# Both delta-rule chains in the same beats: a change to the mixer's order, the stick-breaking sums, two boundary rows and the last adds

## The chip, the cores and the metric

The kernel runs on one core of one Trainium2 chip. The metric is the device time of one execution in microseconds (us), with the median taken over several executions. Engines are named as the profile does: PE is TensorE, DVE VectorE, ACT ScalarE, POOL GpSimd, SP SyncE (here it issues the weight transfers).

## The reference

All matrices are fp32. The input is x, 512 tokens of 1024 channels, and a memory of 256 tokens. Six sublayers follow one another, each as h = h + rmsnorm(y) with y computed from rmsnorm(h):

```
y = hybrid_mixer(rmsnorm(h))            # 4 heads of the gated delta rule, and a conv branch
y = memory_cross_attention(rmsnorm(h), rmsnorm(mem))
y = conv_glu_ffn(rmsnorm(h))
y = retention_chunkwise(...) @ w_out
y = stick_breaking_attention(...) @ w_out     # keys and values from the state before
```

The mixer projects h to queries, keys and values (short conv, silu), gates, decay logits and the conv branch:

```
u, w   = triangular_solve(I + L, ...)   # per chunk of 64 tokens
v_new  = u - w @ S
o      = (q * exp(g)) @ S + attn @ v_new
S      = S * exp(g_last) + (k decayed)^T @ v_new
o      = rmsnorm(o) * silu(gate)
c      = causal_dwconv(glu(cfm), 31 taps); c = silu(layernorm(c))
y      = concat(o, c) @ w_out
```

Stick-breaking weighs key s for query t by sigmoid(z_ts) times the product of (1 - sigmoid(z_tj)) over the keys between them, so it needs suffix sums of log(1 - sigmoid(z)) along the keys.

## The kernel before

**Slabs.** All weights stream as 257 slabs of 128x1024 fp32 (512 KB). SP loads a slab into one of three raw buffers, ACT casts its high part to fp32r (`ahead`, L1280, into one of four buffers sh), DVE forms the low part raw minus high (`low`, L1984, buffers sl), and PE multiplies with the activations, also kept as a high and a low part, in three products per pair of tiles (L499, L500, L501; other places through `one`, L504). The buffer sh of slab n is that of slab n + 4, so the cast of slab n + 4 waits until PE has used slab n. Activations have 512 columns (tokens), or 256 for the memory.

**The order.** Each engine has its own program, and the programs meet at semaphores. The order is written by hand. Side work stands in generators, put into queues (bg, fg, side; gp and tp for taps), and `beat()` at fixed places of each slab runs every queue on to its next `yield`: one tick. A slab over 512 columns has 3 beats, after 9, 18 and 24 of its 24 matmuls; a memory slab 1. `drain()` runs a queue to its end at once.

**The mixer.** 20 slabs make queries, keys and values (12, wqkv) and the conv branch (8, wcfm), then KEYS_GATES follows: eight memory-key slabs mk (256 columns) and four gate slabs, slabs 20 to 31; then slabs 32 to 39 for the memory's values, in `tokens` (the mem tokens are stationary), and the output from slab 40. The delta rule works on two pairs of heads, p = 0 and 1, each a `chain(p)`: transposes, the products of each 64-token chunk, doubling levels of the triangular inverse in tiles of 64x64 (32 PE records for each set), u and w, then eight states, in which S (`ss`) passes from chunk to chunk between PE and DVE. Chain 0 starts after slab 5 and chain 1 after slab 14. `gdn_out(p)` norms a pair of heads: ACT squares, a DVE add, an fp32 PE sum by ONE over sq (128x512), ACT Ln and Exp, DVE scaling.

**Taps.** The conv branch has four channel groups c, each with 31 taps, one a tick. Groups 0 and 2 are made by ACT, which scales a shifted copy into ca0 or ca1 (L1466), and POOL, which adds it to acc (L2976); tap q may be scaled only when the add q-2 is done. Groups 1 and 3 are made by DVE in one instruction a tap, in PSUM (L2194). Group 0 starts after slab 7 and group 2 follows it in the same queue; `mk` slabs tick this queue twice. The queue is drained after slab 31.

**Boundaries.** `boundary(b)` sits between sublayers b and b + 1: y is normed and added to h, h is squared and summed, and its reciprocal root RB, a row of 512 values over all partitions, is needed to scale the next products. Before, PE makes 20 sums of one column with ONE as the moving tile, DVE forms the mean and a diagonal, POOL the power, PE a row by ONE times the diagonal over 512 columns, and DVE copies it to RB.

**Stick-breaking.** For four values of p with two heads each, `weights(p, h)` makes scores, softplus `sp` with high part `split` and low part `spl`, and per block of 128 keys s a suffix sum with the masks LWR (triangle) and ONR (ones), each in a bank of its own; `sp` of the last block enters in fp32.

Of the kernel before, what the change touches and what calls it, by code (L numbers as in the profile page):

```python
# [9 lines left out]
ALU = mybir.AluOpType  # L10
# [156 lines left out]
def program(nc, A, out):  # L167
    root = ExitStack()
    with root:
# [42 lines left out]
        with ExitStack() as ph:  # L212
# [14 lines left out]
            SS = alloc(ph, "ss", [128, 2, 128])  # L227
# [32 lines left out]
        with ExitStack() as ph:  # L260
# [11 lines left out]
            ONR = alloc(ph, "onr", [128, 128], F32R)  # L272
# [87 lines left out]
        def sig(n, step=1):  # L360
# [13 lines left out]
        zero, hvp, yr = sig("zeroed"), sig("h_pool"), sig("y_rstd")  # L374
        cv, cva = sig("conv_tap"), sig("conv_act")
# [16 lines left out]
                   x2h, x2l, sq, sa, cs, ms, pw, dg, rw, rb, hs, zero, hvp, yr, cv, cva, wabh, wabl, lgt, lgp, dcv, dca, vtp, vts,  # L392
# [13 lines left out]
        ONB = ((4, 3), (6, 7))  # L406
        TAP_BANKS, TAP_HOP = (2, 5), 12
        CVB = (0, 1, 2, 3, 5, 0, 0, 1, 0, 1, 0, 1)
# [7 lines left out]
        def tap_sum(c, q):  # L416

            return ACC[:, c, :] if q == 30 else PS[TAP_BANKS[0] if c == 1 and q < TAP_HOP else TAP_BANKS[1]][:]
# [36 lines left out]
        GLB = ((1, 2), (0, 1), (0, 1), (0, 1))  # L455
# [17 lines left out]
        Y_ADD = (1, 2)  # L473

# [10 lines left out]
        def tensor_program(e):  # L485
# [99 lines left out]
            def h_sum(b, k, hf, first):  # L585
# [10 lines left out]
                for tb in range(2):  # L596
# [14 lines left out]
            for _ in range(8):  # L611
                one(PS[7][:, 0:256], SS[:, 0, :], SS[:].rearrange("p a b -> p (a b)"), True, True)
# [68 lines left out]
            def chain(p):  # L681
# [103 lines left out]
                for n in range(8):  # L785
                    tb, par = n // 2, n % 2
                    R, RO = RR[par], RR[1 - par]
                    b = bank(6 + par)
                    pe.wait_ge(*gac[(p, "wq", par)])
                    pe.wait_ge(*(gdv[(p, "s", n - 1)] if n else ggp[(p, "s0")]))  # L790
                    for h in range(2):
                        g = (h * 8 + n) * 128
                        t = one(b[:, h * 128:h * 128 + 128], W2[:, g:g + 128], SS[:, h, :], h == 0, False)
# [15 lines left out]
                    rel[6 + par] = [(gac, (p, "tok", n))]  # L809
                    yield  # L810
                for h in range(2):
                    b = bank(6 + h)
# [5 lines left out]
                rel[6], rel[7] = [(gac, (p, "ot", 0))], [(gac, (p, "ot", 1))]  # L818

            def mem():  # L820
                b = bank(3)
# [6 lines left out]
                rel[3] = [(ms, "mem")]  # L828
# [3 lines left out]
                one(bank(3)[:, 0:256], ONE[:], DG[:, 0:256], True, True).then_inc(*rw("mem"))  # L832
                rel[3] = [(rb, "mem")]
# [9 lines left out]
            bg.add(chain(0))  # L843
# [2381 lines left out]
```

## Time and profile before

| | us |
|---|---|
| median of 3 runs | 1701.21 |
| lowest and highest | 1700.98, 1704.16 |
| the profiled execution | 1702.69 |
| its span in the profile | 1700.9 |
| mean granted TensorE clock | 0.997 |
| PE busy | 1679.8 |
| DVE busy | 1051.8 |
| ACT busy | 733.3 |
| POOL busy | 191.6 |

The rows further down come from this one execution; times in them count from its span's start. Matmuls are pipelined, so the duration of one is longer than its distance to the next; distances between starts say what it costs. An fp32 matmul shows as two records.

### The profile page before, as it was taken

To read this page: it belongs to the slowest core of one execution; us is meant where nothing else is said; L and a number is where in the kernel's file an instruction comes from. 1 tells how busy PE (TensorE), PEld (TensorE's weight loads), DVE (VectorE), ACT (ScalarE), POOL (GpSimd) and SP (SyncE) were. 2 spreads that over 40 slices of the span, in tenths; PEclk is the share of its full clock that TensorE was granted. 3 is DMA by queue.
4 is the path that set the end of the run, shared out by engine and by line. 5 is a ranking of instruction groups with operands and counts; after the bars stand their busy time and mean duration, and the time that the engine had idled before them with its cause. 6 is when DMAs were issued, how large, how long until landed. Compare 5 with 4: busy or idle time off the path is not lost.

```text
span 1700.9 us, 23339 instructions
## 1 busy us (share of the span) xinstructions
PE 1679.8 (99%) x9481; PEld 1410.6 (83%) x9481; DVE 1051.8 (62%) x1574; ACT 733.3 (43%) x1125; POOL 191.6 (11%) x165
## 2 busy tenths in 40 slices
PE   9999999999999999999999999999999999999997
PEld 7787887987898888888888888888898888888886
DVE  7889787474389449549575642655475545364545
ACT  6654467643543223213543323323364655353462
POOL 0455461200210000000100000000100000000001
PEclk9999999999999999999999999999999999999999
DMA  6211134421123323323322313213212222222221
GB/s 217 63 39 63 51 100 134 139 75 50 64 73 112 111 75 112 99 80 106 118 88 78 98 53 106 100 64 110 72 62 87 63 86 75 87 75 85 76 74 50
DMA packets 45578, 147.70 MB, mean 87 GB/s; under 512 B 5024, under 2 KB 8992, under 8 KB 45472
## 3 DMA queue, kind: packets, MB, share of 16 engines
q1 hardware_dynamic: 45472, 146.21, 25.9%
q8 instruction: 76, 1.25, 0.3%
q14 instruction: 30, 0.25, 0.0%
HBM read 144.09 MB, written 2.10 MB: 86 GB/s over the span
## 4 chain that ended last, share of the span: by engine, by line
PE 89%; DVE 8%; issue 1%; ACT 1%; POOL 0%; DVEq 0%; ACTq 0%; POOLq 0%
PE ps L499 22%; PE ps L504 22%; PE ps L501 22%; PE ps L500 22%; DVE sl L1984 1%; DVE y L2399 1%; DVE ps L2044 1%; DVE xl L2416 1%; DVE h L2409 0%; PE ps L1119 0%; DVE ps L2194 0%; DVE ps L2038 0%; DVE pad L2036 0%; ACT xh L1325 0%; ACT sh L1280 0%
## 5 line engine op out<-in xcount | busy, mean ns | idle before, releaser
L1280 ACT ACTIVATE sh<-raw 128x1024 fp32r<-128x1024 f32 x257 | 268.0, 1053 | 381.5 <-PE ps L501 256.2
L1984 DVE TENSOR_TENSOR sl<-raw,sh 128x1024 fp32r<-128x1024 f32 x257 | 321.3, 1258 | 126.2 <-ACT sh L1280 126.1
L499 PE MATMUL ps<-xh,sh 128*128 128x512 f32 (+1 forms) x664 | 264.8, 399 | 0.0
L501 PE MATMUL ps<-xl,sh 128*128 128x512 f32 (+1 forms) x664 | 254.3, 383 | 0.0
L500 PE MATMUL ps<-xh,sl 128*128 128x512 f32 (+1 forms) x664 | 254.2, 383 | 0.0
L499 PE MATMUL ps<-sh,xh 128*128 128x512 f32 x384 | 152.5, 397 | 0.0
L500 PE MATMUL ps<-sh,xl 128*128 128x512 f32 x384 | 149.6, 390 | 0.0
L501 PE MATMUL ps<-sl,xh 128*128 128x512 f32 x384 | 149.6, 390 | 0.0
L499 PEld LDWEIGHTS ps<-xh,sh 128*128 128x128 f32 x664 | 125.1, 188 | 27.0 <-issue 3.3
L501 PEld LDWEIGHTS ps<-xl,sh 128*128 128x128 f32 x664 | 125.1, 188 | 25.0
L500 PEld LDWEIGHTS ps<-xh,sl 128*128 128x128 f32 x664 | 125.3, 189 | 23.0 <-issue 1.2
L2907 POOL TENSOR_TENSOR dg<-dg,sq 128x512 f32<-128x512 f32 (+1 forms) x27 | 30.1, 1113 | 816.5 <-ACT sq L1286 815.1
L499 PE MATMUL ps<-x2hu,sh 128*128 128x256 f32 (+1 forms) x346 | 118.9, 344 | 0.0
L501 PE MATMUL ps<-x2lu,sh 128*128 128x256 f32 (+1 forms) x346 | 115.9, 335 | 0.0
L500 PE MATMUL ps<-x2hu,sl 128*128 128x256 f32 (+1 forms) x346 | 115.1, 333 | 0.0
L499 PE MATMUL ps<-x2hd,sh 128*128 128x512 f32 (+1 forms) x300 | 104.2, 347 | 0.0
L501 PE MATMUL ps<-x2ld,sh 128*128 128x512 f32 (+1 forms) x300 | 102.4, 341 | 0.0
L500 PE MATMUL ps<-x2hd,sl 128*128 128x512 f32 (+1 forms) x300 | 102.0, 340 | 0.0
L2976 POOL TENSOR_TENSOR acc<-acc,ca 128x512 f32<-128x512 f32 x60 | 86.1, 1435 | 70.4 <-ACT ca L1466 65.9
L501 PEld LDWEIGHTS ps<-sl,xh 128*128 128x128 f32 x384 | 72.1, 188 | 15.5
L499 PEld LDWEIGHTS ps<-sh,xh 128*128 128x128 f32 x384 | 72.1, 188 | 15.3 <-issue 0.5
L500 PEld LDWEIGHTS ps<-sh,xl 128*128 128x128 f32 x384 | 72.2, 188 | 15.2 <-issue 0.5
(418 smaller groups left out, 3337.5 us busy)
## 6 DMA issues: line engine op xcount, KB each, us to landing
raw<-in_wup SPq DMA_DIRECT2D x44, 512.0 KB, 3.5
raw<-in_wdn SPq DMA_DIRECT2D x24, 512.0 KB, 3.5
raw<-in_rqk SPq DMA_DIRECT2D x16, 512.0 KB, 3.9
raw<-in_rv SPq DMA_DIRECT2D x16, 512.0 KB, 3.5
raw<-in_rg SPq DMA_DIRECT2D x16, 512.0 KB, 4.7
raw<-in_rout SPq DMA_DIRECT2D x16, 512.0 KB, 3.5
raw<-in_sv SPq DMA_DIRECT2D x16, 512.0 KB, 3.4
raw<-in_sg SPq DMA_DIRECT2D x16, 512.0 KB, 3.4
```

Source lines behind the costliest of these rows:

```text
L499: e.matmul(dst, wh, ah, start=start, stop=False, skip_group_check=True)
L500: e.matmul(dst, wl, ah, start=False, stop=False, skip_group_check=True)
L501: return e.matmul(dst, wh, al, start=False, stop=stop, skip_group_check=True)
L504: return e.matmul(dst, a, b, start=start, stop=stop, skip_group_check=True)
L1280: e.activation(SH[j % NSPL][:], RAW[j % NRAW][:], ACT.Copy).then_inc(*hi(j))
L1984: e.tensor_tensor(SL[j % NSPL][:], RAW[j % NRAW][:], SH[j % NSPL][:].bitcast(F32), ALU.subtract).then_inc(*lo(j))
L2044: e.scalar_tensor_tensor(C[:], PAD[:, 1 + q:1 + q + T], prm("gconv", tile * 4 + q), C[:], ALU.mult, ALU.add).then_inc(*cv((n, "t", q) if q ...
L2399: e.scalar_tensor_tensor(Y[:, k, c], Y[:, k, c], prm(gpost[0], gpost[1] + k), YR[:, c], ALU.mult, ALU.mult).then_inc(*yv(("y", b, "n", k, ...
L2416: e.scalar_tensor_tensor(lo_[:, k, c], H[:, k, c], prm(g[0], g[1] + k), hi_[:, k, c].bitcast(F32), ALU.mult, ALU.subtract).then_inc(*s2((k ...
L2907: e.tensor_tensor(SA[:, c], SA[:, c], SQ[(k - 1) % 2][:] if k < 4 else half(SQ, k % 4), ALU.add).then_inc(*sa(("y", b, k)))
L2976: e.tensor_tensor(ACC[:, c, :], ACC[:, c, :], gpb[("tmp", c, q)], ALU.add).then_inc(*tpp((c, q)))
```

## The change

There are five parts.

1. **Order of the weights.** All 12 wqkv slabs come first (0 to 11), then the 8 wcfm slabs (12 to 19). Both chains are added after slab 10 and tick in the same beats, 37 ticks each. Each has its state `SSP[p]` and its own PSUM banks. Both are drained before slab 29, and both `gdn_out` are queued there; before, `gdn_out(0)` was queued before slab 30, chain 1 was drained after slab 31 and `gdn_out(1)` queued then.
2. **Taps** follow the wcfm slabs: group 0 starts after slab 13 (before 7), group 1 after 15 (before 9), group 2 behind group 0 in the same queue, group 3 after slab 19.
3. **Stick-breaking sums.** They run from s = 2 to 0 in one bank that keeps its sum, with the masks UPR (one minus LOW) and LWR; DVE reads the bank between two steps, and PE waits for that. `weights(p)` holds both heads of p, with a tick between the steps.
4. **Rows at boundaries 1 and 2** (H_ROW). PE makes the row at once, 10 fp32 sums by ONE over 256 columns, and ACT does Ln and Exp straight into RB. The one-column sums, the diagonal, the fp32 row and the copy go there.
5. **The last adds.** Of the second half's eight residual adds POOL does k = 0, 2, 4, PE k = 1, 3, 5 (IDN times h plus IDN times y, fp32, ACT copies the sum out), DVE 6 and 7; before, POOL did three and DVE five.

Over the whole program PE has 8481 matmuls where it had 8519, ACT 15 instructions more (among them four more loads of its function table), DVE 9 less, POOL 2 less.

The core of the diff:

```diff
     for p in range(2):
         o += [("wqkv", j * 4 + 2 * p + h) for j in range(3) for h in range(2)]
-        for c in (2 * p, 2 * p + 1):
-            o += [("wcfm", 4 + c), ("wcfm", c)]
+    for c in range(4):
+        o += [("wcfm", 4 + c), ("wcfm", c)]
...
+            SSP = [alloc(ph, f"ss{i}", [128, 2, 128]) for i in range(2)]
...
+        TAP_BANK, JOIN, HEADS_OUT = 7, 10, 9
...
+        OUT_POOL, OUT_PE = (0, 2, 4), {1: 1, 3: 2, 5: 4}
+        H_ROW = (1, 2)
...
+                if b in H_ROW:
+                    t = one(bank(7)[:, 0:256] if hf else PS[4][:, 0:256], ONE[:], hsq(k), first, k == (0 if hf else 6))
...
             slab(5, X, "x", beats=3, at_bank=[0])
             rel[0] = [(cva, conv_tile(5))]
-            bg.add(chain(0))
+            for n in range(6, 12):
+                slab(n, X, "x", beats=3, at_bank=[CVB[n]])
+                rel[CVB[n]] = [(cva, conv_tile(n))]
+                if n == JOIN:
+                    bg.add(chain(0))
+                    fg.add(chain(1))
...
-            glu(0, 6)
+            glu(0, 12)
             side.add(mem())
-            glu(1, 8)
-            rel[TAP_BANKS[0]] = [(tpd, (1, TAP_HOP))]
-            for n in range(6, 12):
-                slab(4 + n, X, "x", beats=3, at_bank=[n % 2])
-                rel[n % 2] = [(cva, conv_tile(n))]
-                if n == 10:
-                    fg.add(chain(1))
+            glu(1, 14)
             glu(2, 16)
             glu(3, 18)
...
             for i, (kind, n) in enumerate(KEYS_GATES):
-                if i == 10:
+                if i == HEADS_OUT:
+                    bg.drain()
+                    fg.drain()
                     side.add(gdn_out(0))
+                    side.add(gdn_out(1))
...
-            fg.drain()
-            fg.add(gdn_out(1))
...
+            def sums(p, h):
+                b, b3 = bank(4), bank(5)
+                last = SP[:, SOFF[3]:]
...
+                one(b[:, 384:T], ONE[:], last, True, False)
+                for s in (2, 1, 0):
+                    pe.wait_ge(*sta[("sh", p, h)])
+                    pe.wait_ge(*stv[("sl", p, h)])
+                    if s < 2:
+                        pe.wait_ge(*stv[("c", p, h, s + 1)])
+                    for q, m in ((s + 1, UPR), (s, LWR)):
+                        for part in (SPLIT, SPL) if q < 3 else ():
...
+            def h_rstd(b, hf):
...
+                e.activation(RB[:, TH[hf]], PS[7 if hf else 4][:, 0:256], ACT.Ln, scale=1.0 / 1024, bias=EPB[:]).then_inc(
...
+                e.activation(RB[:, TH[hf]], RB[:, TH[hf]], ACT.Exp, scale=-0.5).then_inc(*yr(("h", b, hf)))
...
+            for k, i in OUT_PE.items():
+                pe.wait_ge(*hv[(4, k, 1)])
+                one(bank(i)[:, 0:256], IDN[:], H[:, k, TH[1]], True, False)
```

Three places show what the change makes of the order. On PE in the mixer, before, one interruption of the slab products (ss and u_xq belong to chain 0's state, u_rq, u_r and u_t to chain 1's inverse):

```order
L504 MATMUL ps<-ss,u_xq 128x128 x2
L504 MATMUL ps<-u_rq,u_r 64x64 x16
L499 MATMUL ps<-xh,sh 128x512
L500 MATMUL ps<-xh,sl 128x512
L501 MATMUL ps<-xl,sh 128x512
```

And after, with both chains at the same level of the inverse (u_xq, u_x, km are chain 0's):

```order
L507 MATMUL ps<-u_xq,u_x 64x64 x16
L507 MATMUL ps<-u_rq,u_r 64x64 x16
L502 MATMUL ps<-xh,sh 128x512
L503 MATMUL ps<-xh,sl 128x512
L504 MATMUL ps<-xl,sh 128x512
```

Pieces of unlike kind stood together before; now the same piece of both chains does.

On ACT at the end of the key and gate slabs, before. The first row of sh is the cast of slab 33, the next ones that of slabs 34 and 35 and so on; the four rows of qk are chain 1's last copies:

```order
L1280 ACTIVATE sh<-raw 128x1024
L1421 ACTIVATE qk<-ps 64x2x128
L1435 ACTIVATE qk<-ps 128x4x64 x4
L1545 ACTIVATE sq<-qk 128x512 x2
L1280 ACTIVATE sh<-raw 128x1024
L1553 ACTIVATE dg<-ps,epq 128x512
```

After, from the cast of slab 34 over that of 35 to that of 36:

```order
L1306 ACTIVATE sh<-raw 128x1024
L1623 ACT_TABLE_LOAD
L1623 ACTIVATE gt<-gt 128x512
L1502 ACTIVATE ca<-cp,prm 128x512 x2
L1306 ACTIVATE sh<-raw 128x1024
L1502 ACTIVATE ca<-cp,prm 128x512 x16
L1580 ACTIVATE sq<-qk 128x512 x2
L1306 ACTIVATE sh<-raw 128x1024
```

Sixteen taps (ca) stand between the cast of slab 35 and the squares of heads 2 and 3 (sq from qk). On PE the sum over those squares, before, stands behind 18 matmuls of slab 32:

```order
L499 MATMUL ps<-sh,x2hu 128x512
L500 MATMUL ps<-sh,x2lu 128x512
L501 MATMUL ps<-sl,x2hu 128x512
L504 MATMUL ps<-sq,one 128x512 x2
L499 MATMUL ps<-sh,x2hu 128x512
```

After, it stands behind the first six matmuls of slab 32, the last memory-key product (x2hu, x2lu of 256 columns) being ahead of those:

```order
L504 MATMUL ps<-x2lu,sh 128x256
L502 MATMUL ps<-sh,x2hu 128x512
L503 MATMUL ps<-sh,x2lu 128x512
L504 MATMUL ps<-sl,x2hu 128x512
L502 MATMUL ps<-sh,x2hu 128x512
L503 MATMUL ps<-sh,x2lu 128x512
L504 MATMUL ps<-sl,x2hu 128x512
L507 MATMUL ps<-sq,one 128x512 x2
```

On PE in the stick-breaking stage, before, the sums of s = 0 and s = 1 in one tick:

```order
L504 MATMUL ps<-split,lwr 128x512
L504 MATMUL ps<-split,onr 128x384
L504 MATMUL ps<-split,onr 128x256
L504 MATMUL ps<-spl,lwr 128x512
L504 MATMUL ps<-spl,onr 128x384
L504 MATMUL ps<-spl,onr 128x256
L504 MATMUL ps<-sp,one 128x128
L504 MATMUL ps<-split,lwr 128x384
L504 MATMUL ps<-split,onr 128x256
L504 MATMUL ps<-spl,lwr 128x384
L504 MATMUL ps<-spl,onr 128x256
L504 MATMUL ps<-sp,one 128x128
```

After, the sums of s = 3 and 2, of 1, and of 0, with twelve slab products between each:

```order
L507 MATMUL ps<-sp,lwr 128x128
L507 MATMUL ps<-sp,one 128x128
L507 MATMUL ps<-split,lwr 128x256
L507 MATMUL ps<-spl,lwr 128x256
...
L507 MATMUL ps<-split,upr 128x256
L507 MATMUL ps<-spl,upr 128x256
L507 MATMUL ps<-split,lwr 128x384
L507 MATMUL ps<-spl,lwr 128x384
...
L507 MATMUL ps<-split,upr 128x384
L507 MATMUL ps<-spl,upr 128x384
L507 MATMUL ps<-split,lwr 128x512
L507 MATMUL ps<-spl,lwr 128x512
```

A block's sum is now added to what the bank holds, and is not made anew for each s.

## Rows read from the trace of the kernel before

**Rows 1.** The page: busy us of engines; the chain that ended last.

```profile
PE 1679.8 (99%) x9481; PEld 1410.6 (83%) x9481; DVE 1051.8 (62%) x1574; ACT 733.3 (43%) x1125; POOL 191.6 (11%) x165
PE 89%; DVE 8%; issue 1%; ACT 1%; POOL 0%; DVEq 0%; ACTq 0%; POOLq 0%
```

**Rows 2.** PE's waits: who waited for whom, us in total, times, longest.

```profile
PE ps L504 <- DVE sl L1984: 1.7, 4, 0.8
PE ps L701 <- DVE u_xq L2099: 1.3, 1, 1.3
...
PE ps L504 <- DVE km L2111: 1.1, 1, 1.1
```

**Rows 3.** Timeline of PE, stick-breaking sums: start us, us, instruction.

```profile
1313.93 0.28 PE L504 MATMUL ps<-spl,lwr 128*128 128x256 f32 x1
1314.05 0.38 PE L504 MATMUL ps<-sp,one 128*128 128x128 f32 x2
1314.27 0.39 PE L504 MATMUL ps<-sp,lwr 128*128 128x128 f32 x2
```

**Rows 4.** Timeline of PE, first boundary.

```profile
362.26 0.50 PE L504 MATMUL ps<-one,acc 128*128 128x1 f32 x4
362.62 0.36 PE L499 MATMUL ps<-xh,sh 128*128 128x256 f32 x1
...
365.75 1.13 PE L504 MATMUL ps<-dg,one 128*128 128x512 f32 x2
...
366.94 0.40 PE L500 MATMUL ps<-xh,sl 128*128 128x512 f32 x1
```

**Rows 5.** Timeline of DVE, one of the last adds.

```profile
1694.20 0.41 DVE L2877 TENSOR_TENSOR h<-h,y 128x256 f32<-128x256 f32 x1
```

**Rows 6.** Timeline of PE: slab matmuls around one set of 32 records, and around two.

```profile
72.67 0.39 PE L501 MATMUL ps<-xl,sh 128*128 128x512 f32 x1
...
74.40 0.39 PE L500 MATMUL ps<-xh,sl 128*128 128x512 f32 x1
...
75.33 0.40 PE L501 MATMUL ps<-xl,sh 128*128 128x512 f32 x1
...
78.01 0.40 PE L500 MATMUL ps<-xh,sl 128*128 128x512 f32 x1
```

**Rows 7.** Timeline of PE behind w; busy us by engine in 120:121, PEclk (0.50).

```profile
115.49 3.74 PE L504 MATMUL ps<-km,u_xq 64*128 64x64 f32 x32
...
119.75 0.63 PE L500 MATMUL ps<-xh,sl 128*128 128x512 f32 x1
120.00:121.00 1.00, 1.00 (x3) 0.74 (x3) 0.00 (x0) 1.00 (x3) 0.00 (x0) 0.50 0.67 270
```

**Rows 8.** POOL's tap adds: ns min/median/max, first and last start; last row: timeline.

```profile
L2976 POOL TENSOR_TENSOR acc<-acc,ca x2: 1281/1289/1297, 225.2 to 226.7; 128x512 f32<-128x512 f32 x2
L2976 POOL TENSOR_TENSOR acc<-acc,ca x2: 1292/1294/1297, 247.5 to 248.9; 128x512 f32<-128x512 f32 x2
247.46 12.53 POOL L2976 TENSOR_TENSOR acc<-acc,ca 128x512 f32<-128x512 f32 x7 [3.35 <-ACT ca L1466]
```

**Rows 9.** Timeline of PE: slab 32 begins, the output begins.

```profile
267.56 0.48 PE L499 MATMUL ps<-sh,x2hu 128*128 128x512 f32 x1
...
292.93 0.40 PE L504 MATMUL ps<-x2hd,sh 128*128 128x512 f32 x1
```

**Rows 10.** Timeline of ACT: a tap, a cast.

```profile
256.13 0.72 ACT L1466 ACTIVATE ca<-cp,prm 128x512 f32<-128x512 f32 x1 [0.62 <-POOL acc L2976]
265.04 1.05 ACT L1280 ACTIVATE sh<-raw 128x1024 fp32r<-128x1024 f32 x1
```

**Rows 11.** Timeline of DVE: a tap, x2ld of k = 3, a low part.

```profile
251.76 0.76 DVE L2194 SCALAR_TENSOR_TENSOR ps<-cp,prm,ps 128x512 f32<-128x512 f32 x1
...
296.88 0.68 DVE L2326 TENSOR_TENSOR x2ld<-gt,x2hd 128x512 fp32r<-128x512 f32 x1
...
303.06 1.22 DVE L1984 TENSOR_TENSOR sl<-raw,sh 128x1024 fp32r<-128x1024 f32 x1
```

More of the change, by code:

```diff
@@ L416, in tap_sum @@
         def tap_sum(c, q):
[L418 removed]
+            return ACC[:, c, :] if q == 30 else PS[TAP_BANK][:]
         RS = (DG[:], PAD[:, 0:T])
@@ L1191, in values @@
+                yield from sums(p, 1)
             def values(p, h):
@@ L1233, in tensor_program @@
                 bg.drain()
-                for part in (weights, values):
-                    for h in range(2):
-                        bg.add(part(p, h))
+                bg.add(weights(p))
+                for h in range(2):
+                    bg.add(values(p, h))
                 j += 4
@@ L1486, in scalar_program @@
             ahead(10)
-            bg.add(chain(0))
+            conv_act(4)
+            beat(3)
+            conv_act(5)
+            for n in range(6, 12):
+                beat(2)
+                ahead(n + 5)
+                if n == JOIN:
+                    bg.add(chain(0))
+                    fg.add(chain(1))
+                beat()
+                conv_act(n)
             def glu(c, j):
-                if c == 0:
-                    conv_act(4)
-                beat(2 if c == 2 else 3)
+                beat(2 if c == 0 else 3)
                 ahead(j + 5)
-                if c == 0:
-                    conv_act(5)
                 ac.wait_ge(*glv[(c, "sg")])
@@ L1501, in glu @@
                     gp.add(taps_gp(c))
-            glu(0, 6)
+            glu(0, 12)
             side.add(mem())
-            glu(1, 8)
-            for n in range(6, 12):
-                beat(2 if n > 6 else 3)
-                ahead(9 + n)
-                if n == 10:
-                    fg.add(chain(1))
-                beat()
-                conv_act(n)
+            glu(1, 14)
             glu(2, 16)
@@ L1930, in scalar_program @@
                 bg.drain()
-                for part in (weights, values):
-                    for h in range(2):
-                        bg.add(part(p, h))
+                bg.add(weights(p))
+                for h in range(2):
+                    bg.add(values(p, h))
                 j += 4
@@ L2228, in vector_program @@
             conv(4, 4, 5, beat)
-            bg.add(chain(0))
             conv(5, 5, 0, beat)
             low(9)
+            for n in range(6, 12):
+                beat(2)
+                if n == JOIN:
+                    bg.add(chain(0))
+                    fg.add(chain(1))
+                conv(n, n, CVB[n], beat)
+                low(n + 4)
             def glu(c, j):
@@ L2253, in glu @@
                     tp.add(taps(c))
-            glu(0, 6)
+            glu(0, 12)
             side.add(mem())
-            glu(1, 8)
-            for n in range(6, 12):
-                beat(2 if n > 6 else 3)
-                if n == 10:
-                    fg.add(chain(1))
-                conv(n, 4 + n, n % 2, beat)
-                low(8 + n)
+            glu(1, 14)
             glu(2, 16)
@@ L2827, in vector_program @@
                 bg.drain()
-                for part in (weights, values):
-                    for h in range(2):
-                        bg.add(part(p, h))
+                bg.add(weights(p))
+                for h in range(2):
+                    bg.add(values(p, h))
                 j += 4
@@ L2993, in pool_program @@
             beat(3)
-            bg.add(chain(0))
-            for c in range(2):
+            for n in range(6, 12):
+                beat(3)
+                if n == JOIN:
+                    bg.add(chain(0))
+                    fg.add(chain(1))
+            for c in range(4):
                 beat(6)
@@ L3000, in pool_program @@
                     gp.add(taps(c))
-            for n in range(6, 12):
-                beat(3)
-                if n == 10:
-                    fg.add(chain(1))
-            for c in (2, 3):
-                beat(6)
-                if c in ON_GP:
-                    gp.add(taps(c))
-            bg.drain()
             side.drain()
```

288 lines of the change are left out of this document (172 added, 116 removed).

## Prediction

> **What bounds the kernel now.** I read the page's busy shares and its chain first. TensorE is busy 99% of the span and carries 89% of the chain that ended last, DVE 8% [rows 1]. So one matmul less is worth its start-to-start time, and an edit on another engine is worth something only where TensorE waits for it. The list of TensorE's waits [rows 2] says where it does: no entry is over 1.7 us, and those of the mixer are a few tenths to 1.3 us each. A gain can thus come only from fewer or better placed TensorE instructions; a loss can come from anything that makes this full engine wait. The sum below is made against the profiled execution, 1702.69 us (span 1700.9), which lies 1.5 us over the median of the runs shown, 1701.21; I apply the difference to the median.
>
> **The sums of stick-breaking attention.** Each of the 8 pairs of (p, head) loses two fp32r matmuls of N=256, 16 in all, and two fp32 matmuls of N=128, which the trace shows as two records each, 32 of the 48 records in all. In that dense stretch [rows 3] a 256-wide fp32r matmul takes 0.12 us from start to start (1313.93 to 1314.05) and a pair of fp32 records 0.22 (1314.05 to 1314.27). 16 x 0.12 + 16 x 0.22 = 1.9 + 3.5 = **-5.4 us**. All of it lies on TensorE, which has no gap there. The new order makes TensorE wait for a DVE subtraction between two steps of one bank, but a tick of slab matmuls stands between them now; a wait there is priced at 0, and at worst at 0.3 us for each of 24 steps, which is the size of one of the small waits of [rows 2], 7 us: that would undo the gain and is an end of the range.
>
> **Rows of the first two boundaries.** Each loses the fp32 row over 512 columns: from the first of two records at 365.75 to the slab's second matmul at 366.94 are 1.2 us [rows 4], of which 0.23 are the slab's first matmul; with the late start before it (0.18) that makes 1.15. Two boundaries: -2.3. Ten sums of 256 columns stand for 20 of one column; four one-column records hold the stream from 362.26 to 362.62 and make the next matmul start later, 0.45 with the rest of that switch; a 256-wide fp32 matmul is two records of about 0.2. 10 x 0.45 - 10 x 0.40 = -0.5. Together **-2.8 us**.
>
> **The end.** DVE does 3 of the second half's residual adds less, each 0.34 (from 1694.20 to the next start, 1694.54) to 0.41 us in the stretch that ends the program [rows 5]: **-1.2 us**. The adds that go to TensorE stand after its last slab, where it has nothing else, and the copies are ACT's, which is idle there; the last transfer stays.
>
> **Merging the two chains.** The chains' small matmuls interrupt the stream of slab matmuls. One set of 32 records of 64x64, which stands between the slab matmuls of 72.67 and 74.06, moves the next one to 74.40: 1.73 us where two steps are 0.46, so 1.27 us [rows 6]. Two such sets in a row, between 75.33 and 78.01, cost 2.68 - 0.46 = 2.2 [rows 6], so the second adds 0.95, and 0.3 is the change of shape out and back. Counted in the two orders, the stream of the mixer is interrupted 59 times for the chains before and about 35 times after, as both chains now tick together. Two unlike shapes in one interruption still change shape between them and save little, two of one shape save up to the 0.3. 24 x 0.3 = 7.2 is the upper end, 0 the lower; I take **-4 us**, since about half of the interruptions that go were already of mixed kind.
>
> **What the merging costs.** At the chain's start TensorE waits 1.3 us for u_xq and 1.1 us for km [rows 2], each for one chain's DVE work; that work (a low part, two copies, sums and a key product for each chain) is now there twice in a row. Were all of both waits doubled it would be 4.8 us; DVE has the copies of the first chain done while TensorE is still in the slab, so I take 4.3 where there were 2.4 to 2.5: **+1.8** (0 to +4). The work of 64 x 128 tiles at 115.49 takes 3.74 us with an array half used; the granted clock falls from 1.00 to 0.50 behind it, from full to the lower of TensorE's two levels, 1.2 GHz, and three slab matmuls fill the microsecond from 120 to 121 at 0.50 [rows 7], where each would take 0.23 at the full clock; six run so, 1.2 us lost. After the change this tick of both chains stands back to back, 7.4 us, and its neighbours double too: **+2** (0 to +5).
>
> **The last taps of the mixer, the large term.** Convolution taps of channel groups 0 and 2 are made by ACT (scale, into one of two buffers) and POOL (add). Before, their generator starts after slab 7 and its 62 ticks are over within the key and gate slabs: POOL's last adds start at 247.46 and end 12.53 us later, at 260.0 [rows 8], TensorE begins the first mem-value slab at 267.56 [rows 9]. After the change it starts after slab 13. From there to the end of the key and gate slabs there are 6 x 3 + 8 x 2 + 4 x 3 = 46 ticks, and 62 - 46 = **16 taps are left**; ACT's order shows them in one piece, behind the cast of slab 35 and ahead of the squares of heads 2 and 3. That cast needs the buffer of slab 31, so it cannot start before TensorE ends slab 31; call this moment T0. ACT then pays 1.05 for the cast and 0.72 for the first tap [rows 10]; with two buffers tap q waits for POOL's add q-2, and POOL's adds start 1.4 to 1.5 us apart when nothing holds them (225.2 to 226.7, 247.5 to 248.9) [rows 8]; I take 1.44. Fourteen adds are 20.2 us, the 16th tap 0.7 [rows 10], the first square 0.6 and DVE's add onto it 0.7, both of the tap's size: T0 + 24. TensorE's order has the sum over those squares behind 6 matmuls of slab 32, at T0 + 1.4, and everything behind it is in order. It waits **22.6 us**. Cast and low part of slab 36 stand behind the same taps, but are needed only 11 us later. The ends of this price: POOL's adds at the shortest duration, 1.28 [rows 8], give 20.3 us, at the mean spacing of a full stretch, 12.53 us for 7 [rows 8], 27.5 us.
>
> Those seven adds are 1.79 us apart in the mean, where DVE has its own work, and 1.4 to 1.5 us at best [rows 8]. The Trainium skill, "SBUF — State Buffer", section "SBUF: two separate sides", says that a DVE instruction with two SBUF inputs and a GpSimd instruction that reads SBUF hold a common port exclusively, the other one waiting it out. By that rule the adds would take the long spacing only while DVE works; DVE itself has run dry in this wait, so the rule speaks for the short one.
>
> What is late next: DVE has to do 7 taps of group 3 after the wait, which it did not have there before (5.2 us at 0.75 [rows 11]), against 3.3 us (two scalings, a low part, a product) that are already behind it; before, it was ready 0.8 us ahead of TensorE (x2ld ends 297.56, used 24 matmuls after the output's first at 292.93, about 298.4) [rows 9, 11]. So **+1.1** (0 to +4, ACT reloads its function table more often there, 1.28 us each). After such a wait the matmuls may start at the half clock, as in [rows 7]: 1.2 us for six of them, **+1.5** with the fp32 sums among them (0 to +3). The Trainium skill, "TensorE: Matmul & The Clock Gate", section "What's actually happening", gives the idle array the lower of two clocks, which would make this cost certain; the rows show the fall only behind half used work.
>
> **Sum.** -5.4 - 2.8 - 1.2 - 4 = -13.4. +1.8 + 2 + 22.6 + 1.1 + 1.5 = +29.0. Net **+15.6 us: 1716.8 us**.
>
> **Rivals.** (a) The taps do not stop TensorE: were POOL and ACT ahead of their ticks, or the squares' sum late enough, only DVE's extra load would remain. From slab 26 to the fourth output product DVE has 31 taps (23 us at 0.75), 14 low parts (16 us at 1.2 less their overlap [rows 11]) and 22 us of norms and products, 62 to 64 us, where TensorE needs 54 (four mem-key slabs of 2.9, two gates of 5.5, 25.4 us of token slabs and sums [rows 9], 5.5 of the output, the rest chain work), so 8 to 10 us stay: -13.4 + 1.8 + 2 + 9 = -0.6, 1700.6 us, no change. Against it: ACT's and TensorE's orders are fixed and the buffers are two. 8%. (b) The late taps are covered altogether and the clock costs nothing: -13.4 + 1.8 = -11.6, about 1690 us, faster. It needs DVE not to be the bound in a stretch where it had 0.8 us in hand [rows 9, 11]. 5%. (c) Slower still: POOL is behind when the key slabs begin, because the chains' products and memory sums now share its queue with the first 18 taps, and in the key slabs two ticks in 2.9 us just equal two adds. Each add that it is behind lengthens the wait by 1.44; with 5 adds behind, or with adds at the long spacing, +5 to +7, and with the clock's upper end 1726 us. It decides when POOL's queue is still full at the first key slab. 15%. (d) The merging does nothing for TensorE (0 instead of -4) or the sums wait: 1721 to 1723. Inside the forecast's range.
>
> **How the numbers follow.** The forecast with its bounds (wait 20.3 to 27.5, merging 0 to -7, clock 0 to 5 and 0 to 3) reaches from 1709 to 1725 and holds 72%. Rivals (a) and (b) hold 13%, (c) 15%. The range from 1707 to 1726 takes in the forecast and half of (c). A measurement of this kernel tells 0.2%, 3.4 us, from no change: slower by more has 0.72 + 0.15 = 0.87, within it 0.07, faster 0.06.
>
> **What would show it.** In the trace of after: one TensorE wait of 20 to 25 us, ahead of an fp32 sum over sq of 128x512, early in the first mem-value slab, released by DVE behind ACT's squares; 16 taps in a row on ACT, each waiting for POOL. Busy time of TensorE down by about 13 us. The stick-breaking stage 5 us shorter. If that wait is missing or under 10 us, the forecast is wrong in its largest term; if it is there and the total is under 1707, the gains were larger than I count them.

## The result

The changed kernel takes 1730.94 us, median of 4 runs (1730.01 to 1732.39), where before takes 1701.24: a ratio of 1.0172, 95% interval 1.0158 to 1.0187, 29.6 us slower (27 to 32). The forecast was 1716.8 with a range up to 1726. The sign and the place of the largest loss were right, the size was half.

The profiled execution took 1732.39 us. The page, busy us and the chain that ended last, where [rows 1] are those of before:

```profile
PE 1681.6 (97%) x9421; PEld 1413.3 (82%) x9421; DVE 1056.9 (61%) x1565; ACT 745.4 (43%) x1140; POOL 183.9 (11%) x163
PE 85%; DVE 8%; ACT 3%; issue 2%; POOL 1%; DMA 0%; SPq 0%; DVEq 0%; POOLq 0%; ACTq 0%
```

TensorE does not work less by its busy time (1681.6 against 1679.8), although it has fewer matmuls: parts of it run at the lower clock (the mean granted clock is 0.985, before 0.997). It now waits. TensorE's waits, us in total, times, longest, which answer to [rows 2]:

```profile
PE ps L507 <- DVE sq L2373: 29.4, 3, 26.5
PE ps L706 <- DVE u_xq L2165: 3.6, 1, 3.6
PE ps L507 <- DVE sl L2050: 2.7, 5, 1.0
PE ps L507 <- DVE sq L2358: 1.5, 1, 1.5
PE ps L507 <- DVE spl L2820: 1.2, 1, 1.2
```

The timeline of TensorE at the end of the mixer (start, us, instruction, idle before it and who ended it):

```profile
263.17 0.39 PE L504 MATMUL ps<-xl,sh 128*128 128x512 f32 x1
265.92 1.10 PE L507 MATMUL ps<-sq,one 128*128 128x512 f32 x2 [2.36 <-DVE sq L2373]
267.60 1.86 PE L507 MATMUL ps<-sq,one 128*128 128x512 f32 x2 [0.58 <-DVE sq L2373]
268.47 1.42 PE L502 MATMUL ps<-xh,sh 128*128 128x512 f32 x1
...
271.54 0.28 PE L502 MATMUL ps<-x2hu,sh 128*128 128x256 f32 x1
...
274.41 0.40 PE L502 MATMUL ps<-sh,x2hu 128*128 128x512 f32 x1
...
275.57 0.39 PE L504 MATMUL ps<-sl,x2hu 128*128 128x512 f32 x1
302.43 3.40 PE L507 MATMUL ps<-sq,one 128*128 128x512 f32 x4 [26.47 <-DVE sq L2373]
305.19 0.86 PE L502 MATMUL ps<-sh,x2hu 128*128 128x512 f32 x1
```

Slab 32 begins at 274.41 (before: 267.56, [rows 9]). Six matmuls later TensorE stands for 26.47 us. The chain of work that ended last, in order of time, says through whom it goes. It starts behind the late squares' sum of heads 0 and 1:

```profile
267.60 1.88 PE ps L507 x2
269.49 0.69 ACT pad L1588
...
271.79 1.06 ACT sh L1306
272.88 1.28 ACT L1623
274.17 0.46 ACT gt L1623
274.71 0.72 ACT ca L1502
275.50 1.30 POOL acc L3065
276.93 2.07 POOL acc L3065
...
299.02 1.27 POOL acc L3065
300.32 0.72 ACT ca L1502
301.04 0.53 ACT sq L1580
301.59 0.70 DVE sq L2373
302.43 3.40 PE ps L507 x4
```

POOL's adds, one after the other, then ACT's last tap, its square, DVE's add, the sum: the path that was forecast. POOL's timeline shows the whole run (start, us, count, idle before it), which answers to [rows 8]:

```profile
275.50 27.91 POOL L3065 TENSOR_TENSOR acc<-acc,ca 128x512 f32<-128x512 f32 x18 [2.29 <-ACT ca L1502]
```

The adds grouped by line in two stretches: from 283.88 on, where DVE has two instructions left and runs dry at 287.90, and before slab 32, where it works (ns min/median/max, first and last start):

```profile
L3065 POOL TENSOR_TENSOR acc<-acc,ca x11: 1263/1265/2059, 283.9 to 299.0; 128x512 f32<-128x512 f32 x11
L3065 POOL TENSOR_TENSOR acc<-acc,ca x13: 1286/1297/2089, 242.9 to 271.9; 128x512 f32<-128x512 f32 x13
```

Eighteen adds and not sixteen: two taps of the key slabs' own ticks were late, since ACT, ahead of them, had stood for TensorE's sums of slab 30 (1.98 us until 267.05 and 1.75 us until 269.49).

The other parts of the change. The timeline of TensorE in the sums of the stick-breaking stage, against [rows 3]:

```profile
1345.33 0.38 PE L507 MATMUL ps<-sp,lwr 128*128 128x128 f32 x2
1345.54 0.39 PE L507 MATMUL ps<-sp,one 128*128 128x128 f32 x2
```

The timeline of DVE at its last work, against [rows 5]:

```profile
1722.84 3.21 DVE L2464 SCALAR_TENSOR_TENSOR y<-y,prm,ps 128x256 f32<-128x256 f32 x8
1725.98 0.74 DVE L2970 TENSOR_TENSOR h<-h,y 128x256 f32<-128x256 f32 x2
```

An fp32 pair costs 0.21 us still. DVE ends with eight norms and two adds where adds stood between the norms. At the first boundary the two records of [rows 4] at 365.75 are gone, and with them the wait of 1.1 us for qx, which ended at 370.03.

### The profile page after: what moved, and what is told of

Same layout as the page of the kernel before. It is cut to its first block, busy times and chain, and to the rows that moved or that the text cites. A ratio compares the mean times of both kernels' runs of the same rounds, so it can differ in the third digit from the quotient of the medians.

```text
span 1729.9 us, 23249 instructions
## 1 busy us (share of the span) xinstructions
PE 1681.6 (97%) x9421; PEld 1413.3 (82%) x9421; DVE 1056.9 (61%) x1565; ACT 745.4 (43%) x1140; POOL 183.9 (11%) x163
## 4 chain that ended last, share of the span: by engine, by line
PE 85%; DVE 8%; ACT 3%; issue 2%; POOL 1%; DMA 0%; SPq 0%; DVEq 0%; POOLq 0%; ACTq 0%
PE ps L502 21%; PE ps L504 21%; PE ps L503 21%; PE ps L507 21%; DVE sl L2050 2%; POOL acc L3065 1%; DVE y L2464 1%; DVE ps L2110 1%; DVE xl L2481 1%; ACT sh L1306 0%; DVE ps L2259 0%; DVE h L2474 0%; PE ps L1127 0%; DMA acc<-in_xT 0%; DVE u_xq L2086 0%
## 5 line engine op out<-in xcount | busy, mean ns | idle before, releaser
L502 PEld LDWEIGHTS ps<-xh,sh 128*128 128x128 f32 x664 | 126.2, 190 | 26.5 <-issue 2.3
L504 PEld LDWEIGHTS ps<-sl,xh 128*128 128x128 f32 x384 | 72.1, 188 | 15.6
```

What stands on the lines that cost most here:

```text
L502: e.matmul(dst, wh, ah, start=start, stop=False, skip_group_check=True)
L504: return e.matmul(dst, wh, al, start=False, stop=stop, skip_group_check=True)
```

## The experiments

**Which part loses.** Runs are named e1 to e15, each name standing at its measurement. Two kernels divide the diff: the three small parts on before's mixer, and the new mixer (order, joint chains, taps) on before's rest.

> Before's mixer, with the new stick-breaking sums, the new rows at boundaries 1 and 2 and the new last adds. The prediction's terms give -5.4 - 2.8 - 1.2 = -9.4 us against before, 1691.8. The traces of before and after put the start of the mixer's output at 292.93 and 333.13, 40.2 us apart, while the whole is 29.7 us apart, so by them these three parts are worth -10.5: 1690.7. A rival in which the sums wait for DVE (the trace of after has one new wait of 1.2 us for spl) gives 1694 or more.

Measured (e1): 1692.92 us, ratio 0.9951 (0.9936 to 0.9966), 8.3 us faster than before (10.9 to 5.8), 1.1 short of the smaller of the two estimates. The reading of 333.13 as the start of the output was wrong; it begins at 329.61, 36.7 us after before's, and the matmul at 333.13 is a later one that waits. The whole is 29.0 us longer by the spans, so by that reading the small parts' share is 7.7. But waits of the mixer's output lie behind that point. The first common point behind them is a slab matmul that waits 0.35 and 0.36 us for DVE's low part, at 340.39 in before and at 378.48 in after. They are 38.1 apart, and the share is 9.1.

> The mixer's new order alone, everything behind it as before. If the parts only add, +40 us: 1741. If the loss of the mixer is given back in part later, under 1738.

Measured (e2): 1740.09 us, ratio 1.0226 (1.0211 to 1.0241), +38.5. The two parts add within the noise: 38.5 - 8.3 = 30.2 against 29.6.

**The small parts alone.** Part 3 of the change on the kernel before, which has the masks and the order of the sums; its core:

```diff
-                for s in range(NB):
...
+                for s in (2, 1, 0):
...
+                    for q, m in ((s + 1, UPR), (s, LWR)):
```

> Before with the new stick-breaking sums alone. 16 x 0.12 + 16 x 0.22 = 5.4 us less: 1695.9. With the new wait for spl (1.2 us in the trace of after) 1697.

Measured (e8): ratio 0.9975 (0.9964 to 0.9986), 4.3 us faster.

Part 4 alone on the kernel before:

```diff
+        H_ROW = (1, 2)
...
+                if b in H_ROW:
+                    t = one(bank(7)[:, 0:256] if hf else PS[4][:, 0:256], ONE[:], hsq(k), first, k == (0 if hf else 6))
```

> Before with the new rows at boundaries 1 and 2 alone. My term is 2 x 1.15 + 0.5 = 2.8 us less: 1698.5. The three small parts together gave 8.4 less and the sums alone 3.3 to 4.3, so rows and end are worth 4 to 5 together: 1698 here.

Measured (e11): ratio 0.9973 (0.9962 to 0.9983), 4.6 us faster.

Part 5 alone on the kernel before:

```diff
+        OUT_POOL, OUT_PE = (0, 2, 4), {1: 1, 3: 2, 5: 4}
...
+            for k, i in OUT_PE.items():
+                ac.wait_ge(*out_ps[k])
+                e.activation(H[:, k, TH[1]], PS[i][:, 0:256], ACT.Copy).then_inc(*hva(k))
```

> Before with the new last adds alone. Three DVE adds of 0.34 to 0.41 us less: 1.2 us less, 1700.1. If the fp32 sums on TensorE and ACT's copies come later than DVE's adds did, no change.

Measured (e12): ratio 0.9993 (0.9984 to 1.0001), 1.2 us faster, not told from nothing. The sum, 10.1, is within the interval of the three together.

**The taps that are left over.** In the programs of ACT and POOL the taps' queue is ticked more than once in a beat of slabs 14 to 19:

```diff
+        GP_TICKS = (1, 2, 2, 2)
...
-                    gp.tick()
+                    for _ in range(per[0]):
+                        gp.tick()
...
+                per[0] = GP_TICKS[c]
```

> The changed kernel, but the queue of the ACT and POOL taps is ticked twice in each beat of slabs 14 to 19 (18 ticks more), so that no tap is left when the key and gate slabs end. Theory (the left over taps): the wait of 26.5 us in slab 32 goes, and with it the half clock behind it; 1702 to 1704. Rival (DVE is behind by 8 to 10 us in this stretch anyway, the taps only cover it): a wait of 8 to 10 us stays in the token slabs or at the output, 1710 to 1713. Rival (POOL is full from slab 14 on, the taps slow the chains): new waits in slabs 14 to 19, over 1713.

Measured (e3): 1712.14 us (1708.58 to 1715.76), ratio 1.0066 (1.0045 to 1.0087): 18 us of the loss are gone, and a wait stays at the same instruction:

```profile
279.07 1.19 PE L508 MATMUL ps<-sq,one 128*128 128x512 f32 x1 [8.33 <-DVE sq L2378]
```

So the taps left over made 26.5 - 8.3 = 18 us of the wait, and behind them something else is late. The prediction's rival with DVE's own work, worked out there at 8 to 10 us, has the size of it; what it is made of is the question of the next runs.

> The same with the double tick in slabs 14 and 15 only (6 ticks more): 10 taps are left in place of 16. Theory: a tap left costs what POOL's adds take from start to start, 1.41 to 1.67 us in the trace of after, so 8.5 to 10 us less: 1721 to 1722.5, wait 17 to 18. If the wait hangs on something else (DVE, the squares), it moves by much less than 8 us.

Here `GP_TICKS` is (1, 2, 1, 1). Measured (e4): 1722.71 us, ratio 1.0123 (1.0108 to 1.0138), 8.3 us less than the changed kernel, and a wait of 18.7 in place of 26.5: 1.3 to 1.4 us for each of the six taps, near the distance of POOL's adds where DVE is idle, 1.41.

**DVE's queue.** DVE's own taps go twice a beat in slabs 16 to 19:

```diff
-                beat(3 if c % 2 else 2)
+                beat(3 if c % 2 else 2, 2 if c > 1 else 1)
...
-                beat(3)
+                beat(3, 2 if c > 1 else 1)
```

> Like the run with two ACT and POOL taps a beat, and DVE's taps too go twice a beat in slabs 16 to 19 (12 ticks, 9 us of DVE work moved to where DVE is busy for 34 of 50 us). Theory (two causes, one behind the other: first the taps left over for POOL, then DVE's own queue): the wait of 8.3 us in slab 32 and the 2.9 us in slab 30 go, 1699 to 1702. Rival (the 8.3 us come from the squares' place in the order, not from DVE's load): 1709 or more.

Measured (e5): 1710.36 us, ratio 1.0040 (1.0026 to 1.0054). The wait in slab 32 is 6.09 and not gone, and the 2.9 us in slab 30 are all there. The theory missed. The rival's 1709 is reached by the median but not by the ratio, which on before's 1701.2 is 1708.0. DVE's taps are a part (8.33 - 6.09 = 2.2 us of the wait), not the rest of it.

The same two lines of DVE's program, without the change to ACT's and POOL's:

> The changed kernel with only DVE's taps twice a beat in slabs 16 to 19; POOL's 16 taps are left as they are. Theory of two nested causes: the 2.9 us in slab 30 go, the wait in slab 32 stays at 25 to 28 us: 1727 to 1729. Rival (DVE's load is the cause of the whole wait): under 1722.

Measured (e6): 1731.35 us, ratio 1.0163 (1.0149 to 1.0177), with a wait of 26.45. DVE's taps alone change nothing while POOL's hold the sum. The 2.9 us in slab 30 stay here too (2.37 and 0.58), against what was expected. The trace of the run before it (both kinds of taps twice a beat) shows what DVE does ahead of them:

```profile
248.71 0.42 DVE L2412 TENSOR_TENSOR km<-ps,cm 128x256 f32<-128x256 f32 x1 [1.52 <-PE ps L505]
...
258.70 2.15 DVE L2055 TENSOR_TENSOR sl<-raw,sh 128x1024 fp32r<-128x1024 f32 x1
260.77 1.54 DVE L2264 SCALAR_TENSOR_TENSOR ps<-cp,prm,ps 128x512 f32<-128x512 f32 x2
262.22 0.42 DVE L2412 TENSOR_TENSOR km<-ps,cm 128x256 f32<-128x256 f32 x1
262.55 1.97 DVE L2055 TENSOR_TENSOR sl<-raw,sh 128x1024 fp32r<-128x1024 f32 x1
264.44 3.42 DVE L2378 TENSOR_TENSOR sq<-sq,q 128x512 f32<-128x512 f32 x2
```

The low part takes up to 2.15 us and two adds onto the squares 3.42, beside POOL's adds; where POOL is silent they take 1.22 and 1.29 (next trace). DVE's instructions from PSUM (the taps, 0.75) keep their duration. It is not a backlog: DVE stood idle for 1.52 us before 248.71 here, and for 1.46 us before 248.27 in the trace of after. What makes it late arises in the 19 us behind that, in which it has ten taps in both kernels and never stops. Beside POOL the two adds are 2.1 us longer and the last two low parts 1.7, together more than the 2.9 us waited. Without the late taps the wait is gone (see work left out); whether the ten taps or the slowing is to blame was not told apart by a run.

**Work left out.** These kernels leave out taps: 16 of group 2's 31, or 28 of the 31 of groups 2 and 3 both. What they compute of the conv branch is incomplete, and no time of theirs is one that a complete kernel could have; they are read for what holds TensorE.

```diff
+        SKIP = (0, 0, 28, 28)
...
+                    if 1 <= j <= SKIP[c]:
+                        continue
```

First `SKIP = (0, 0, 16, 0)`, with all 31 taps of group 3:

> The changed kernel with 16 of the 31 taps of channel group 2 left out (ACT and POOL), so that none is left over, and POOL and ACT have less work in all. Theory (the left over taps, then DVE's own queue behind them): the wait in slab 32 falls from 26.5 to 6 to 9 us, as in the run with two ticks a beat: 1708 to 1712. If POOL's adds slow DVE a good deal (the low part takes 1.2 us alone and up to 2.15 beside them), less: 1704 to 1708.

Measured (e9): 1713.16 us, ratio 1.0060 (1.0047 to 1.0073). The wait is 10.41, above the 6 to 9 expected and the 8.33 of two ticks a beat, although POOL has less to do. The time agrees with that run's (1.0066).

Then, as in the diff, 28 of each:

> The changed kernel with 28 of the 31 taps of channel groups 2 and 3 left out, which takes 40 us of POOL's and 21 us of DVE's work out of the end of the mixer. What is left is the joint chains and the three small parts. Theory (the late taps are nearly the whole loss): no wait over 1 us behind slab 20; 1731 - 26.5 - 2.9 - 1.5 - 1 - 2 to 3 for the clock = 1696 to 1697, which is 3 to 5 us over the run with the three small parts alone (1692.9): that much is the joint chains' loss. Rival (the order of the heads' norms holds TensorE whatever the load): a wait of 5 us or more stays, 1702 or more.

Measured (e10): ratio 0.9994 (0.9985 to 1.0003), and a wait of 4.02 us in slab 32. The theory missed (no wait over 1 us), and the rival is right in part (5 us or more): with neither POOL nor DVE loaded, something still holds the sum. Its DVE rows:

```profile
264.20 0.42 DVE L2412 TENSOR_TENSOR km<-ps,cm 128x256 f32<-128x256 f32 x1 [1.03 <-PE ps L505]
264.54 1.22 DVE L2053 TENSOR_TENSOR sl<-raw,sh 128x1024 fp32r<-128x1024 f32 x1
265.67 0.75 DVE L2383 SCALAR_TENSOR_TENSOR qk<-qk,prm,dg 128x512 f32<-128x512 f32 x1
266.33 0.75 DVE L2383 SCALAR_TENSOR_TENSOR qk<-qk,prm,pad 128x512 f32<-128x512 f32 x1
266.99 1.22 DVE L2053 TENSOR_TENSOR sl<-raw,sh 128x1024 fp32r<-128x1024 f32 x1
268.13 0.69 DVE L2391 TENSOR_TENSOR gt<-qk,gt 128x512 f32<-128x512 f32 x1
268.73 1.29 DVE L2378 TENSOR_TENSOR sq<-sq,q 128x512 f32<-128x512 f32 x2
```

Slab 32 begins at 263.99. DVE waits for the end of slab 31 at 264.20, and from there on runs without a gap through what stands in its order, until the first of the two adds onto the squares ends at about 269.4. TensorE's six matmuls are over at 265.5. By this reading the place of the sum alone makes the 4 us of wait. To test that, the sum is moved back to where it stood before, 18 matmuls into slab 32:

```diff
             def gdn_out(p):
                 yield
                 yield
+                for _ in range(2 * p):
+                    yield
                 for h in range(2):
```

> The same later sum in the kernel without 28 taps each of groups 2 and 3 (they are left out). There a wait of 4.0 us was left although DVE was busy for 12 of 25 us: its low part of slab 35 waits for ACT's cast, that for TensorE's end of slab 31, and the adds onto the squares stand behind it. If that place is the cause of the 4.0 us, they fall to 1.3 and the time by 2.7: 0.2% under the kernel before. If the wait stays as long, the cause is elsewhere.

Measured (e14): ratio 0.9961 (0.9949 to 0.9973), 5.6 us faster than without the move, where 2.7 was expected; the wait falls to 1.30 as expected. The two traces show the rest. The output begins 34.2 us behind slab 32 without the move and 26.9 with it. Of these 7.3 us, 2.7 are the wait, 1.5 the wait for the next sum (0 with the move), and about 3 a stretch at the lower clock from 269 to 276, behind the wait of 4 us, which the other trace does not have.

The same move in the changed kernel, with all its taps:

> The changed kernel with one thing moved: TensorE's sum over the squares of heads 2 and 3 stands 18 matmuls into slab 32, as before, and not 6. If only what the sum waits for counts (the 16 taps), TensorE does 12 matmuls of its wait first, so the wait is 2.7 us shorter and these matmuls are not left behind it: 1728. If the queue behind the sum is later in turn (ACT's Ln waits for the sum, casts stand behind it), 1730 to 1731.

Measured (e13): 1727.93 us, ratio 1.0153 (1.0138 to 1.0168); wait 23.2, 3.3 us less. The time is 3.2 less by the ratios, on the side of the first theory (2.7), though their intervals overlap (after: 1.0158 to 1.0187).

**What the joint chains do.** On the kernel with both kinds of taps twice a beat, chain 1 starts three ticks behind chain 0, in all four engines' programs:

```diff
             def chain(p):
                 QK = QKS[p]
+                for _ in range(3 * p):
+                    yield
```

> Like the run with both kinds of taps two a beat, and chain 1 starts three ticks behind chain 0, so that unlike pieces of the two chains stand together and the two w steps no longer stand back to back. If like pieces in one beat save switches (mine: up to 0.3 us each, 4 us in all) this is 2 to 4 us slower than that run. If what the joint steps cost in clock and in waits at the chains' start (3.6 us for u_xq) is larger, it is 1 to 4 us faster.

Measured (e7): 1708.81 us, ratio 1.0032 (1.0019 to 1.0044), against 1.0040 (1.0026 to 1.0054): the intervals overlap, so neither gain nor loss can be told. The wait of 3.6 us for u_xq is gone and one of 3.1 us for ACT's qk has come.

The traces tell apart what the times do not. The table takes the start of slab 32 in each. From it go TensorE's idle time from 5 us on and the time lost to the clock, an estimate: busy time times one minus the granted clock, summed over stretches of 1 us. A slab matmul takes 0.43 us from start to start at the lower clock (269.68 to 270.11 in the trace of after) and 0.23 at the full one, which is what such an estimate supposes. What is left is the work at full clock.

| trace | slab 32 begins | idle | lost to the clock | work |
|---|---|---|---|---|
| before | 267.56 | 5.0 | 1.7 | 260.8 |
| the small parts on before's mixer (e1) | 266.34 | 5.1 | 0.0 | 261.2 |
| after | 274.41 | 8.4 | 11.5 | 254.5 |
| 56 taps left out, sum in its old place (e14) | 265.95 | 6.3 | 5.0 | 254.7 |
| both kinds of taps twice a beat (e5) | 273.23 | 9.2 | 9.6 | 254.5 |
| the same, chain 1 later (e7) | 270.32 | 8.1 | 3.3 | 258.9 |

The work is 260.3 to 261.2 in all five traces with before's mixer and 254.5 to 255.5 in all ten with joint chains. So the joint chains and the new order save about 6 us of work, and about 4 of them (4.4 in this pair) are lost when chain 1 starts three ticks later, as the first theory had it. The clock gives more than that back (9.6 to 3.3) and the waits 1.1, as the second had it: both are right, and they cancel. The clock's part is the less certain one, since it differs between traces of one mixer: 0 to 5.1 us with before's, 4.4 to 11.5 with joint chains.

The last kernel puts all of it together: both kinds of taps twice a beat, chain 1 three ticks later, the sum in its old place. It leaves out nothing.

> The changed kernel with both kinds of taps twice a beat, chain 1 three ticks later and the later sum. The run without the later sum had 6.1 us of wait there and gave 1.0032 of before. 2.7 us less: 1.0016. It would still be 10 us above the three small parts alone (0.9951), and what is left then is what the order of the slabs itself costs in the mixer.

Measured (e15): 1701.92 us, ratio 1.0000 (0.9991 to 1.0010), 5.4 us below the run without the later sum, where 2.7 was expected. As without the taps, the stretch at the lower clock behind the wait (2.5 us lost from 278 to 284) goes with the wait. The three small parts on before's mixer (0.9951) remain 8 us faster, and that run is the fastest complete kernel here.

**The bill.** In us against before, each from two ratios times 1702:

| step | us |
|---|---|
| the three small parts (before to e1) | -8.3 |
| joint chains and new order, 56 taps left out, sum in its old place (e1 to e14) | +1.7, not told from 0 |
| these taps back in, both kinds twice a beat, chain 1 three ticks later (e14 to e15) | +6.6 |
| place of the sum (e15 to e7) | +5.4 |
| chain 1 in the same ticks (e7 to e5) | +1.4, not told from 0 |
| DVE's taps late by up to 12 (e5 to e3) | +4.4, the intervals overlap |
| 16 taps left over (e3 to after) | +18.0 |

These are the steps of one path from before to after, so that their sum, 29.2, must come out at the whole and proves nothing; what each step is worth depends on the order in which they are taken.

## Why the prediction was wrong in size

**Sums, rows, end: right.** -5.4, -2.8 and -1.2 were forecast; -4.3 (-6.1 to -2.4), -4.6 (-6.5 to -2.9) and -1.2 (-2.7 to +0.2) were measured. The sums have one wait for spl, 1.2 us, which is the size of the difference. The rows also took the wait of 1.1 us for qx away, which was priced nowhere; it is gone in the trace of the rows alone too.

**Merging and what it costs: near in sum without the late taps, by two terms that were both too small.** -4 + 1.8 + 2 = -0.2 was forecast, +1.7 measured, which is not told from it. In the table above, the kernel without the 56 taps has 6.5 us less work than the one with the small parts alone (254.7 against 261.2), 1.2 more idle time and 5.0 more lost to the clock. That a saving of 6 and a loss of 6 stand where -4 and +3.8 were written, and cancel again, is luck. An interruption with the two like sets in the trace of after costs

```profile
110.09 0.39 PE L504 MATMUL ps<-xl,sh 128*128 128x512 f32 x1
110.41 1.15 PE L507 MATMUL ps<-u_xq,u_x 64*64 64x64 f32 x32
111.39 1.10 PE L507 MATMUL ps<-u_rq,u_r 64*64 64x64 f32 x32
...
112.75 0.39 PE L503 MATMUL ps<-xh,sl 128*128 128x512 f32 x1
```

2.66 - 0.46 = 2.2 us, as two in [rows 6]: 0.3 less than two single sets, as the prediction had it. Behind the joint w the clock stands at the lower level for longer than in [rows 7]. Windows of TensorE's busy us in the trace of after, the clock being the third number from the right, and the second of the two w steps:

```profile
170.00:175.00 5.00, 5.00 (x44) 5.00 (x43) 0.48 (x1) 1.82 (x4) 0.00 (x0) 0.72 0.01 3
175.00:180.00 5.00, 5.00 (x24) 4.59 (x24) 0.00 (x0) 1.83 (x5) 0.00 (x0) 0.50 0.00 0
172.83 5.60 PE L507 MATMUL ps<-u_t,u_rq 64*128 64x64 f32 x29
```

The second step runs at the lower clock itself: the same 29 records take 3.04 us in the trace of e3, where the clock fell only at their end.

**The arrival at slab 32: the step that failed.** The prediction let TensorE reach slab 32 (T0) at -0.2 us against before, and put DVE's lateness only behind the wait. The trace has T0 at 274.41 against 267.56, +6.9. By the table this is -6.3 of work (-4 forecast), +3.4 of idle time (+1.8) and +9.7 of time lost to the clock (+2).

The clock is the term that was mis-sized most. Where before has one stretch at the lower clock (118 to 122, 1.7 us lost), after has four: 56 to 60 (1.7), 98 to 104 behind the wait of 3.6 us for u_xq (3.0), 172 to 183 in and behind the joint w (5.1), and 267 to 272 behind the waits in slab 30 (1.6). Only the third was priced, at 2. Part of the 9.7 belongs to this execution and not to the change, as the spread over the ten traces says.

Of the idle time, 2.9 us are the waits in slab 30 for DVE's adds onto the squares of heads 0 and 1, which stand in no term. DVE is late there because it runs for 19 us without a gap, its low parts up to 1.8 times and its adds up to 2.7 times as long as where POOL is silent. I had walked DVE's order with 1.15 us for a low part, taken where POOL is silent. Of 20 low parts between 107 and 276 in the trace of after the median takes 1.394 us and the longest 2.156.

**The wait: the mechanism right, the size short by 3.9.** 22.6 was forecast, 26.5 measured, inside 20.3 to 27.5. The price of an add was right where DVE is idle (1.41 from start to start, 290.57 to 291.98 and on). But the prediction had DVE dry in this wait, and it worked until 287.90; until then adds took up to 2.07, and the mean from start to start is 1.55 (275.50 to 300.32 for 16). POOL also had two adds more in front, as ACT had first stood for TensorE's late sums in slab 30. The split of the wait was wrong: I gave it all to the taps. 18 us were theirs; the rest would have been there without them. Rival (a) held 8 to 10 us of DVE's load as an alternative to the taps. It should have been a floor under them; but of the 8.3 us found there, the runs give DVE's taps 2.2 and the place of the sum about 4, and that place is in no term of the prediction.

**Behind the wait: +4.8 where 2.6 stood.** Up to the common point at 340.39 and 378.48, 38.1 - 6.9 - 26.5 leaves 4.8 (rounded from 4.77). The granted clock stood at 0.50 over 280 to 300, in the wait, and the four fp32 records behind it took 2.76 us (305.19 - 302.43), where they take 1.39 at the full one (271.52 to 272.91 in the trace of e14), and waits of 1.5 and 1.0 us follow.

In all, in the traces: -9.1 for the small parts (-9.4), +6.9 for the way to slab 32 (-0.2), +26.5 (22.6), +4.8 (2.6), which is 29.1 for the 29.0 of the spans (15.6). The largest miss, 7.1 of 13.5 us, is the way to slab 32.

## What to carry over

Count what is left in every side queue at the point where it is drained; a `drain` is a hard stop for the engine, and what stands behind it in program order is late by the whole rest. When a wait is explained by one queue, ask what the next one under it would have cost: here three lay one below the other (POOL's taps, DVE's taps, the place of the sum), and removing the upper one gave 18 of 26.5 us. A wait is not over when it ends: in two pairs of traces here 2.5 and 3.0 us were lost at the lower clock behind one and went with it. Where a change makes waits or sets half-filled matmul steps side by side, put a price on each such place, and compare traces by idle time and clock before crediting the order. Walk a dense engine with the durations that it has beside its neighbour, not with those of a quiet stretch. And before moving work that is covered where it stands (here the conv branch's taps), ask what it will stand in front of.

## What the runs showed of the hardware

In the rows seen, POOL and DVE slow each other where both read only SBUF. DVE's low part (two SBUF inputs) takes 1.22 us alone and 1.3 to 2.16 beside POOL's adds, two adds onto squares 1.29 and 3.42, while its taps with one input in PSUM stay at 0.75; POOL's add takes 1.27 where DVE is idle and up to 2.09 beside it. In the prediction I had used this for POOL's side alone, and it is on DVE's side that it reached TensorE. The Trainium skill, "SBUF — State Buffer", section "SBUF: two separate sides", states it for both sides: whichever of the two starts first has the shared port for its whole instruction, and the other waits. The trace agrees in that both are lengthened.

The granted clock in 170:190 differs from trace to trace, though all have the chains joined: 0.74 in after, e5, e6 and e9, 0.83 in e4 and e14, 0.91 in e2, e3, e10 and e13, which is 5.1, 3.4 and 1.7 us lost in the stretch that begins at 171 to 174. With one trace each, kernel and execution are not told apart. But single runs of one kernel show the same: of e3's four runs the two at a mean clock of 0.994 and 0.995 took 1710.06 and 1708.58 us, the two at 0.990 took 1715.76 and 1714.22. The figure of 18.0 us for the taps left over rests on the median of these four, so that its uncertainty is 3 to 4 us; the two traces give 18.1 for the wait itself.
